# Decoder trunk: the loads and splits at three stage borders moved into the stage ahead of each

## The chip, the cores and the metric

The kernel runs on one core of a Trainium2 chip. The metric is the device time of one execution, in microseconds (us); lower is better. Engines are named as in the profile: PE (TensorE), DVE (VectorE), ACT (ScalarE), POOL (GpSimd) and SP, which here issues every DMA.

## The reference, cut to what matters

One layer of a decoder, for a prompt of 2048 rows and for 8 samples of 4 new rows each, with the same weights:

```python
h = rmsnorm(x, w['norm1_g'])
proj = jnp.einsum('nld,dc->nlc', h, w['w_in'])
qa, ka, va, qb, kb, vb, zc = jnp.split(proj, IN_SPLITS, axis=-1)
...
oc, s_fin = rwkv_mixer(zc, z_before, s0, w)      # the recurrence: token shift, decay, delta-rule state
mix = jnp.concatenate([oa.reshape(N, L, A_Q), ob.reshape(N, L, B_W), oc], axis=-1).astype(x.dtype)
x = x + jnp.einsum('nlc,cd->nld', mix, w['w_out'])
u = jnp.einsum('nld,df->nlf', rmsnorm(x, w['norm2_g']), w['mlp_up'])
x = x + jnp.einsum('nlf,fd->nld', jnp.square(jax.nn.relu(u)), w['mlp_down'])
```

The prompt's recurrence starts from a zero state and zero shift row; the samples' starts from `state_c_wkv` and `state_c_shift`.

## The kernel before

The program is a row of stages, each a block of its own: at its end every engine meets the others at a barrier, and SP reaches it only after its last stores have landed. The stages, with the profile's tile names:

1. `project`: the combined projection, written to `projT` and `vtok` in DRAM.
2. `prompt_attention`: attention heads of the prompt; results (`p_mo`) stored to `mixT` in DRAM.
3. A block of its own, `Era.clear` (L54 to L60): SP clears the 67 semaphores that stages 1 and 2 used, so that the later stages can have them.
4. `rwkv` with tag `cp`: the prompt's recurrence, in 8 segments of 256 tokens. Between its own steps the engines run the samples' attention (`SampleAttention`, "side"), whose cached keys and values come in 30 units of 768 KB through a ring of three buffers (`p_ring`).
5. `rwkv` with tag `cs`: the samples' recurrence, a single segment of 32 columns.
6. `out_project`: 17 row tiles times `w_out`, residual, norm, transpose.
7. `mlp`.

In stages 4 and 5 (L1956 to L1961) SP first issues the loads of the rows `z`, then of 14 constants (16 with the samples' row mask and state). All four compute engines wait at their start for every one of these loads (`c_in`), and all but DVE for DVE's preparation of `hbias`, `hka`, `omka` and `rko` as well (`zeroed`, L2001 to L2008). DVE's first consumers wait for POOL's `shift` (L1892, the difference of neighbouring tokens), which needs `z`. The order on each engine is written out by hand: `walk` calls `prepare` in pieces 0 to 10 (all ahead of the first group for segment 0), then `levels_of`, `hop` and `finish`; for the samples `special` follows `levels_of`.

In stage 6 every matmul of fp32 data is three matmuls on a high part (`mh`, `wh`, an ACT copy to fp32r) and a low part (`ml`, `wl`, a DVE subtraction). ACT and DVE split the weights `w_o` in two halves of 2 MB, and the first two tiles of `mixT` (`p_mix`), at the start of the stage, after SP has loaded them; PE waits for the first half (`w_low`).

Of the kernel before, what the change touches and what calls it, by code (L numbers as in the profile page):

```python
# [47 lines left out]
class Era(ExitStack):  # L48
# [351 lines left out]
def prompt_attention(nc, outer, projT, vtok, mask_w, mask_0, sinks, ident, mixT):  # L400
# [21 lines left out]
    with ExitStack() as ctx:  # L422
# [74 lines left out]
        def _(sp):  # L497
# [408 lines left out]
class SampleAttention:  # L906
# [5 lines left out]
    def __init__(self, nc, ctx, outer, projT, vtok, units, mask_b, mask_a, sink_a, ident, mixT):  # L912
        s = Scope(nc, ctx, outer)
        self.NR = NR = 3
        self.units, self.mixT = units, mixT
        self.ring = [s.sb(f"p3_ring{i}", [P, UNIT]) for i in range(NR)]
# [60 lines left out]
    def load_until(self, sp, slot):  # L977

        while self.next_unit < len(self.release):
# [7 lines left out]
            self.next_unit += 1  # L987

# [274 lines left out]
def rwkv(nc, outer, tag, sample, src, shift0, state0, cst, wts, mixT, col0, state_out, side=None):  # L1263
# [17 lines left out]
    with ExitStack() as ctx:  # L1281
        s = Scope(nc, ctx, outer)
        n_ = lambda x: f"{tag}_{x}"
        z = s.sb(n_("z"), [P, NZ, nb, nq + 1])
# [11 lines left out]
        sh0 = s.sb(n_("sh0"), [P, NZ, nb, 1]) if sample else None  # L1296
        znew = s.sb(n_("znew"), [P, NZ, W]) if sample else None
# [3 lines left out]
        par = s.sb(n_("par"), [P, 32])  # L1301
        omka = s.sb(n_("omka"), [P, NP3])
        hka = s.sb(n_("hka"), [P, NP3])
        hbias = s.sb(n_("hbias"), [P, 6])
        w2 = s.sb(n_("w2"), [P, 384])
        g2 = s.sb(n_("g2"), [P, 384])
        hones = s.sb(n_("hones"), [P, P])
        hmean = s.sb(n_("hmean"), [P, P])
        rko = s.sb(n_("rko"), [P, NP3, P])
        id64 = s.sb(n_("id64"), [P, HD])  # L1310
        mAB = s.sb(n_("mAB"), [P, 2, C])
        mT1 = s.sb(n_("mT1"), [P, C])
        mM1 = s.sb(n_("mM1"), [P, C])
        idU = s.sb(n_("idU"), [P, C])
        mL = s.sb(n_("mL"), [P, len(levels), C])
        scm = s.sb(n_("scm"), [P, W])
        cc = s.sb(n_("cc"), [P, 1])
        hsum = s.sb(n_("hsum"), [P, 32])
        hback = s.sb(n_("hback"), [96, NP3, P])
        ksum = s.sb(n_("ksum"), [96, W])  # L1320
        vsum = s.sb(n_("vsum"), [96, W])
        rm = s.sb(n_("rm"), [P, NB]) if sample else None
# [10 lines left out]
        S0 = s.sb(n_("S0"), [P, NS0, NP3, nb, HD])  # L1333
# [4 lines left out]
        c_in = s.sem(n_("c_in"))  # L1338
        z_in = s.sem(n_("z_in"))
        shift_in = s.sem(n_("shift_in")) if sample else None  # L1340
# [8 lines left out]
        consts = [(par[:, :], cst["par"]), (hsum[:, :], cst["hsum"]), (hback[:, :, :], cst["hback"]), (w2[:, :], wts["w2"]), (g2[:, :], wts["g2"]), (hones[:, :], cst["hones"]),  # L1349
                  (hmean[:, :], cst["hmean"]), (id64[:, :], cst["id64"]), (mAB[:, :, :], cst[tag + "AB"]),  # L1350
                  (mT1[:, :], cst[tag + "T1"]), (mM1[:, :], cst[tag + "M1"]), (idU[:, :], cst[tag + "I"]),
                  (mL[:, :, :], cst[tag + "L"]), (scm[:, :], cst[tag + "scan"])]
        if sample:
            consts += [(rm[:, :], cst["rowmask"]), (S0[:, 0], state0)]
# [247 lines left out]
        def scalar_walk(e):  # L1602
# [3 lines left out]
            def prepare(seg, i):  # L1606
# [1188 lines left out]
```

## Time and profile before

| | us |
|---|---|
| median of 3 runs | 3337.21 (3335.07 to 3338.07) |
| the profiled execution | 3336.69 |
| its span | 3334.9 |
| PE busy | 3066.4 (92%) |
| DVE busy | 1581.4 (47%) |
| ACT busy | 816.6 (24%) |
| POOL busy | 351.7 (11%) |

The profile is that of one execution. "Busy" is the sum of an engine's instructions; a row of the timeline says when a group of instructions starts, how long it lasts in all, and in brackets how long the engine had been idle and what ended that.

### The profile page before, as it was taken

How to read it: one execution, taken by the hardware profiler on the slowest of the kernel's cores; microseconds unless marked ns; L12 is line 12 of the kernel's file. 1: busy time of each engine (PE TensorE's matmuls, PEld its weight loads, DVE VectorE, ACT ScalarE, POOL GpSimd, SP SyncE). 2: the span in 40 equal slices, each digit the busy share in tenths (PEclk: the TensorE clock that was granted, in tenths of full speed). 3: DMA queues.
4: the chain of work that ended last, by engine and by line, in shares of the span. 5: the costliest groups of instructions: out<-in, count | busy, mean ns of one | idle time of the engine just before them, and what ended most of it. 6: DMA issues, size and time to landing. Idle time of an engine off the chain costs nothing. (4 is left out here: it accounts for less than half of the span.)

```text
span 3334.9 us, 65660 instructions
## 1 busy us (share of the span) xinstructions
PE 3066.4 (92%) x27080; PEld 2599.7 (78%) x27080; DVE 1581.4 (47%) x3057; ACT 816.6 (24%) x1500; POOL 351.7 (11%) x473
## 2 busy tenths in 40 slices
PE   7999999799589888875699799999999999999998
PEld 7999997466377777764487588888887988888887
DVE  6211121677466666742333444444446554444545
ACT  5000000565222333211222322111123211222112
POOL 4000000643232233210000000000000000000000
PEclk9999999899799999995799899999999999999999
DMA  4222121531322320001454511111113311111111
GB/s 149 71 71 71 68 84 48 156 104 36 98 86 82 117 82 25 7 12 30 142 173 147 182 51 50 50 50 33 42 51 105 131 51 50 50 37 39 50 45 65
DMA packets 145083, 249.58 MB, mean 75 GB/s; under 512 B 21952, under 2 KB 101920, under 8 KB 144096
## 3 DMA queue, kind: packets, MB, share of 16 engines
q1 hardware_dynamic: 144864, 246.41, 22.1%
q8 instruction: 167, 2.74, 0.3%
q14 instruction: 52, 0.43, 0.0%
HBM read 185.85 MB, written 60.52 MB: 74 GB/s over the span
## 5 line engine op out<-in xcount | busy, mean ns | idle before, releaser
L2639 DVE TENSOR_TENSOR m_y<-m_y,m_db 128x512 f32<-128x512 f32 x512 | 351.9, 688 | 324.4 <-PE m_db L2408 324.0
L2406 PE MATMUL m_ub<-m_hh,m_wuh 128*128 128x352 f32 (+1 forms) x1280 | 451.4, 353 | 19.4 <-DVE m_hl L2585 19.4
L2407 PE MATMUL m_ub<-m_hl,m_wuh 128*128 128x352 f32 (+1 forms) x1280 | 449.9, 351 | 0.0
L2408 PE MATMUL m_ub<-m_hh,m_wul 128*128 128x352 f32 (+1 forms) x1280 | 449.4, 351 | 0.0
L2406 PE MATMUL m_db<-m_wdh,m_uh 128*128 128x512 f32 x1024 | 407.3, 398 | 4.8 <-DVE m_wdl L2594 4.7
L2408 PE MATMUL m_db<-m_wdh,m_ul 128*128 128x512 f32 x1024 | 404.3, 395 | 0.0
L2407 PE MATMUL m_db<-m_wdl,m_uh 128*128 128x512 f32 x1024 | 403.2, 394 | 0.0
L186 PE MATMUL p_bank<-p_xh,p_wh 128*128 128x416 f32 x800 | 286.6, 358 | 11.8 <-DVE p_wl L307 11.8
L187 PE MATMUL p_bank<-p_xl,p_wh 128*128 128x416 f32 x800 | 283.8, 355 | 0.0
L188 PE MATMUL p_bank<-p_xh,p_wl 128*128 128x416 f32 x800 | 282.8, 353 | 0.0
L2406 PEld LDWEIGHTS m_ub<-m_hh,m_wuh 128*128 128x128 f32 x1280 | 241.0, 188 | 46.8 <-issue 13.1
L2407 PEld LDWEIGHTS m_ub<-m_hl,m_wuh 128*128 128x128 f32 x1280 | 241.4, 189 | 23.3
L2408 PEld LDWEIGHTS m_ub<-m_hh,m_wul 128*128 128x128 f32 x1280 | 241.0, 188 | 22.8
L2406 PEld LDWEIGHTS m_db<-m_wdh,m_uh 128*128 128x128 f32 x1024 | 192.7, 188 | 63.6 <-issue 19.4
L2607 DVE TENSOR_TENSOR m_sq<-m_r 128x352 f32<-128x352 f32 (+1 forms) x160 | 94.5, 590 | 294.0 <-ACT m_r L2503 294.0
L2408 PEld LDWEIGHTS m_db<-m_wdh,m_ul 128*128 128x128 f32 x1024 | 192.8, 188 | 46.1
L2407 PEld LDWEIGHTS m_db<-m_wdl,m_uh 128*128 128x128 f32 x1024 | 193.4, 189 | 44.6
L2528 ACT ACTIVATE m_wdh<-m_wdr 128x1024 fp32r<-128x1024 f32 x62 | 62.2, 1052 | 630.8 <-PE m_db L2408 630.8
L2503 ACT ACTIVATE m_r<-m_ub 128x352 f32<-128x352 f32 (+1 forms) x160 | 82.8, 517 | 449.4 <-PE m_ub L2408 438.2
L186 PEld LDWEIGHTS p_bank<-p_xh,p_wh 128*128 128x128 f32 x800 | 153.4, 192 | 14.3 <-DVE p_wl L307 12.2
L362 DVE TENSOR_TENSOR p_ob<-p_bank,p_rs 128x416 f32<-128x416 f32 x70 | 41.4, 592 | 256.0 <-PE p_bank L188 256.0
L188 PEld LDWEIGHTS p_bank<-p_xh,p_wl 128*128 128x128 f32 x800 | 152.2, 190 | 2.2
(394 smaller groups left out, 5047.8 us busy)
## 6 DMA issues: line engine op xcount, KB each, us to landing
m_wur<-w_up SPq DMA_DIRECT2D x64, 512.0 KB, 6.1
m_wdr<-w_dn SPq DMA_DIRECT2D x64, 512.0 KB, 4.3
p_ring<-units SPq DMA_DIRECT2D x30, 768.0 KB, 6.2
out_projT<-p_ob SPq DMA_DIRECT2D x100, 208.0 KB, 1.9
cp_z<-out_projT SPq DMA_DIRECT2D x8, 1408.0 KB, 7.8
p_wr<-w_fm SPq DMA_DIRECT2D x20, 512.0 KB, 3.6
p_mix<-mixT SPq DMA_DIRECT2D x16, 512.0 KB, 5.0
p_x<-x SPq DMA_DIRECT2D x16, 512.0 KB, 3.7
```

What stands on the lines that cost most here:

```text
L186: pe.matmul(out, wh_, mh, start=(k == 0), stop=False)
L187: pe.matmul(out, wh_, ml, start=False, stop=False)
L188: return pe.matmul(out, wl_, mh, start=False, stop=(k == KC - 1))
L362: dve.tensor_tensor(ob[gi][:, 0:TG], bank[gi][:, 0:TG], rs[:, cols(gi)], ALU.mult).then_inc(evac, 1)
L2406: pe.matmul(out, wh, mh, start=first, stop=False)
L2407: pe.matmul(out, wh, ml, start=False, stop=False)
L2408: return pe.matmul(out, wl, mh, start=False, stop=last)
L2503: act.activation(r[:, q, 0:n], ub[g][:, 0:n], ACT.Relu).then_inc(relued, 1)
L2528: act.activation(wdh[:, j], wdr[:, j], ACT.Copy).then_inc(wd_high, 1)
L2607: dve.tensor_tensor(sq[:, q, 0:n], r[:, q, 0:n], r[:, q, 0:n], ALU.mult).then_inc(u_sq, 1)
L2639: dve.tensor_tensor(yh, yh, db[(2 * a + h) % ND][:, :], ALU.add).then_inc(y_added, 1)
```

## The change

Three things move, and no arithmetic of the result changes.

- `RwkvShared` holds the prompt's first rows `z` and the constants that both recurrences use, in tiles of their own (`rw_...`). It is loaded by SP inside `prompt_attention`, when that stage has come to its last head pair. The samples' recurrence no longer loads or prepares constants again.
- The block that clears semaphores is gone. SP clears the 67 of stages 1 and 2 inside the prompt's recurrence, in its last segment (`stale.clear`). In the same place `SampleEarly` loads what the samples' recurrence needs of its own (state, rows, shift rows, seven small constants) into two ring buffers whose last units have been used.
- `OutWeights` loads `w_o` in eight parts, and the first two tiles of `mixT`, at the start of the samples' recurrence. ACT makes the high parts after its `prepare` pieces 6 to 9, DVE the low parts in `special`, between `vm` and `um`. `out_project` begins with these done; PE there waits for all eight parts.

```diff
@@ class Era
-    def clear(self):
-        with self.nc.Block() as block:
-            @block.sync
-            def _(sp):
-                for handle in self.held:
-                    sp.sem_clear(handle)
+    def clear(self, sp):
+        for handle in self.held:
+            sp.sem_clear(handle)
@@ prompt_attention, sync
                     load_k(u + 1)
                     load_v(u + 1)
+                else:
+                    shared.load(sp)
                 for c in range(NCL):
                     store(NCL * u + c)
@@ class SampleAttention
+    def load_early(self, sp):
+
+        for n, load in ((len(self.release) - 3, self.early.load_state), (len(self.release) - 2, self.early.load_rest)):
+            sem, count, _ = self.release[n]
+            sp.wait_ge(sem, count)
+            load(sp)
@@ rwkv, scalar_walk, prepare
                     S.done(e.activation(ksum[:, :], ksum[:, :], ACT.Sqrt), "sroot", seg)
+                if i in (6, 7, 8, 9) and ahead and not isinstance(e, Rehearsal):
+                    for k in (2 * i - 12, 2 * i - 11):
+                        ahead.high(e, k)
@@ rwkv, vector_walk, special
                     V.done(i, name, 0)
+                    if name == "vm" and ahead and not isinstance(e, Rehearsal):
+                        for k in range(KC):
+                            ahead.low(e, k)
@@ rwkv, sync
-            if sample:
-                sp.dma_start(znew[:, :, :], src[:, :, SEQ:T].rearrange("z p t -> p z t")).then_inc(z_in, 16)
-                sp.dma_start(sh0[:, :, :, :], shift0).then_inc(shift_in, 16)
-            else:
-                sp.dma_start(z[:, :, 0, 1:nq + 1], src[:, :, 0:W].rearrange("z p t -> p z t")).then_inc(z_in, 16)
-            for dst, src_ in consts:
-                sp.dma_start(dst, src_).then_inc(c_in, 16)
+            if ahead:
+                ahead.load(sp)
...
                     side.load_until(sp, PIECES * (seg - 1) + 1)
+                if side and seg == nseg - 1:
+                    side.load_early(sp)
+                    stale.clear(sp)
@@ class OutWeights
+    def load(self, sp):
+        for k in range(KC):
+            sp.dma_start(self.wr[:, k, :], self.w_o[:, k, :]).then_inc(self.w_in[k], 16)
+        for t in range(2):
+            sp.dma_start(self.m[t][:, :, :], self.mixT[:, :, P * t:P * (t + 1)].rearrange("k p n -> p k n")).then_inc(self.mix_in[t], 16)
+
+    def high(self, act, k):
+        act.wait_ge(self.w_in[k], 16)
+        act.activation(self.wh[:, k, :], self.wr[:, k, :], ACT.Copy).then_inc(self.w_high, 1)
+        if k < 2:
+            act.wait_ge(self.mix_in[k], 16)
+            act.activation(self.mh[k][:, :, :], self.m[k][:, :, :], ACT.Copy).then_inc(self.m_high, 1)
```

How SP's program reads. Before, between the last stores of the attention (`mixT<-p_mo`) and the first loads of the recurrence stand the 67 clears and the branches of three borders:

```order
L531 DMA mixT<-p_mo 128x512 x8
L422 UNCONDITIONAL_BRANCH
L57 UNCONDITIONAL_BRANCH
L60 ISA x67
L56 UNCONDITIONAL_BRANCH
L1949 UNCONDITIONAL_BRANCH
L1959 DMA cp_z<-out_projT 128x11x256
L1961 DMA cp_par<-cst_par 128x32
```

After the change the loads of `z` and the constants stand four stores earlier (the rest of the constants is left out between these two pieces), and the samples' attention's own loads (`p_qa` to `p_ident`, 16 of them) are the first of the new stage:

```order
L528 DMA mixT<-p_mo 128x512 x4
L2048 DMA cp_z<-out_projT 128x11x256
L2050 DMA rw_par<-cst_par 128x32
```

```order
L2050 DMA cp_scm<-cst_cpscan 128x256
L528 DMA mixT<-p_mo 128x512 x4
L419 UNCONDITIONAL_BRANCH
L1937 UNCONDITIONAL_BRANCH
L974 DMA p_qa<-out_projT 64x32 x4
L974 DMA p_qb<-out_projT 128x3x32
```

What moved: 15 loads went ahead of the border, 67 clears and two borders are gone from it. The clears now stand, with ten small loads ahead of them, between the fifth and the sixth of the recurrence's eight stores (`mixT<-cp_yc`).

ACT's program in the samples' recurrence, after the change, from the square root of `prepare` piece 5 to the first copies of `levels_of`:

```order
L1615 ACT_TABLE_LOAD
L1615 ACTIVATE cs_ksum<-cs_ksum 96x32
L2146 ACTIVATE p_wh<-p_wr 128x1024
L2149 ACTIVATE p_mh<-p_mix 128x1024
L2146 ACTIVATE p_wh<-p_wr 128x1024
L2149 ACTIVATE p_mh<-p_mix 128x1024
L2146 ACTIVATE p_wh<-p_wr 128x1024 x6
L1648 ACTIVATE cs_tok<-cs_q 32x192 x6
```

Before, `cs_tok` followed `cs_ksum` directly; ten copies now stand between them, the second of which waits for a tile of `mixT` that SP loads after all eight parts of `w_o`.

DVE's program in `special`, after the change:

```order
L1844 TENSOR_TENSOR cs_vm<-cs_tok,p_ring 32x512 x6
L2153 TENSOR_TENSOR p_wl<-p_wr,p_wh 128x1024
L2156 TENSOR_TENSOR p_ml<-p_mix,p_mh 128x1024
L2153 TENSOR_TENSOR p_wl<-p_wr,p_wh 128x1024
L2156 TENSOR_TENSOR p_ml<-p_mix,p_mh 128x1024
L2153 TENSOR_TENSOR p_wl<-p_wr,p_wh 128x1024 x6
L1844 TENSOR_TENSOR cs_um<-cs_uu,p_ring 32x512 x6
```

Before, `cs_um` followed `cs_vm`; ten subtractions now stand between them.

## Rows read from the trace of the kernel before

**Rows 1.** The page, busy time of the engines.

```profile
PE 3066.4 (92%) x27080; PEld 2599.7 (78%) x27080; DVE 1581.4 (47%) x3057; ACT 816.6 (24%) x1500; POOL 351.7 (11%) x473
```

**Rows 2.** Timeline, attention to prompt's recurrence: start, length, instructions [idle <-releaser].

```profile
866.34 0.32 SPq L531 DMA_DIRECT2D mixT<-p_mo  x1
...
873.35 0.39 SPq L1959 DMA_DIRECT2D cp_z<-out_projT  x1
...
884.57 0.17 DVE L2001 TENSOR_SCALAR cp_hbias<-cp_par 128x6 f32<-128x6 f32 x1 [18.26 <-issue]
...
885.62 4.88 POOL L1892 TENSOR_TENSOR cp_zs<-cp_z 128x2816 f32<-128x2816 f32 x1 [27.78 <-DVE cp_rko L2007]
```

**Rows 3.** Waits of SP's queue: us in total, times, longest us.

```profile
SPq L556 <- DMA mixT<-p_mo: 1.7, 1, 1.7
...
SPq L1281 <- DMA out_state_s<-cs_S: 2.9, 1, 2.9
...
SPq L1953 <- DVE cp_yc L1788: 221.2, 7, 67.8
```

**Rows 4.** Timeline, first segment of the prompt's recurrence.

```profile
889.59 1.38 SPq L986 DMA_DIRECT2D p_ring<-units  x3
...
895.35 0.38 SPq L1968 DMA_DIRECT2D cp_z<-out_projT  x1
...
904.12 4.88 POOL L1892 TENSOR_TENSOR cp_zs<-cp_z 128x2816 f32<-128x2816 f32 x1 [6.33 <-DMA cp_z<-out_projT]
...
907.78 0.42 ACT L1632 ACTIVATE cp_ksum<-cp_ksum 96x256 f32<-96x256 f32 x1
...
909.74 1.74 DVE L1744 RECIPROCAL cp_ksum<-cp_ksum 96x256 f32<-96x256 f32 x1
```

**Rows 5.** Line L1741, all its instructions: ns min/median/max.

```profile
L1741 DVE TENSOR_TENSOR cp_tA<-cp_kp,cp_zs x8: 944/1142/4017, 905.8 to 1395.2; 128x768 f32<-128x768 f32 x8
```

**Rows 6.** Timeline, prompt's to samples' recurrence, and the samples' first steps.

```profile
1505.61 0.37 SPq L1956 DMA_DIRECT2D cs_znew<-out_projT  x1
...
1518.40 0.17 DVE L2001 TENSOR_SCALAR cs_hbias<-cs_par 128x6 f32<-128x6 f32 x1 [18.03 <-issue]
...
1519.51 0.70 DVE L2011 MEMSET cs_am<- 128x768 f32 x1 [0.23 <-DVE cs_rko L2007]
1520.12 0.19 DVE L1704 COPY cs_z<-cs_sh 128x88 f32<-128x88 f32 x1
...
1531.76 0.23 ACT L1632 ACTIVATE cs_ksum<-cs_ksum 96x32 f32<-96x32 f32 x1
...
1540.07 2.01 ACT L1662 ACTIVATE cs_tok<-cs_q 32x192 f32<-32x192 f32 x6 [8.08 <-PE cs_q L1533]
```

**Rows 7.** Lines of the splits in `project`, the same shapes: ns min/median/max.

```profile
L292 ACT ACTIVATE p_wh<-p_wr x16: 1059/1060/1061, 104.5 to 450.7; 128x1024 fp32r<-128x1024 f32 x16
L365 DVE TENSOR_TENSOR p_wl<-p_wr,p_wh x14: 1224/1225/1226, 133.7 to 429.0; 128x1024 fp32r<-128x1024 f32 x14
```

**Rows 8.** Timeline, samples' recurrence to output projection.

```profile
1563.79 3.78 DVE L1859 TENSOR_TENSOR cs_um<-cs_uu,cs_rm 32x512 f32<-32x512 f32 x6 [15.59 <-ACT cs_uu L1681]
...
1601.42 0.48 SPq L1982 DMA_DIRECT2D out_state_s<-cs_S  x1
...
1605.21 0.37 SPq L2097 DMA_DIRECT2D p_mix<-mixT  x1
1605.30 0.06 DVE L2191 MEMSET p_eps<- 128x1 f32 x1 [4.33 <-PEq L1281]
...
1619.52 3.62 ACT L2172 ACTIVATE p_wh<-p_wr 128x4096 fp32r<-128x4096 f32 x1 [1.34 <-DMA p_wr<-w_o]
...
1622.78 0.76 PE L2151 MATMUL p_acc<-p_wh,p_mh 128*128 128x512 f32 x1 [23.44 <-DVE p_wl L2202]
```

**Rows 9.** The page, DMA issues: KB each, us to landing.

```profile
cp_z<-out_projT SPq DMA_DIRECT2D x8, 1408.0 KB, 7.8
```

**Rows 10.** A window's length, then PE, PEld, DVE, ACT, POOL busy (count), then granted clock, DMA share, GB/s.

```profile
1605.00:1622.00 17.00, 0.00 (x0) 0.00 (x0) 5.08 (x3) 7.15 (x3) 0.00 (x0) 0.50 0.94 357
```

More of the change, by code:

```diff
@@ L2045, in rwkv_constants, with __init__, staging, load @@
     return out
-def out_project(nc, outer, mixT, xtok, w_o, g2, ident, x2, h2T):
+class OutWeights:
+    def __init__(self, nc, ctx, outer, mixT, w_o):
+        s = Scope(nc, ctx, outer)
+        self.wh = s.sb("p5_wh", [P, KC, D], F32R)
+        self.wl = s.sb("p5_wl", [P, KC, D], F32R)
+        self.m = [s.sb(f"p5_mix{i}", [P, KC, P]) for i in range(2)]
+        self.mh = [s.sb(f"p5_mh{i}", [P, KC, P], F32R) for i in range(2)]
+        self.ml = [s.sb(f"p5_ml{i}", [P, KC, P], F32R) for i in range(2)]
+        self.w_in = [s.sem(f"p5_w_in{i}") for i in range(KC)]
+        self.w_high = s.sem("p5_w_high")
+        self.w_low = s.sem("p5_w_low")
+        self.mix_in = [s.sem(f"p5_mix_in{i}") for i in range(2)]
+        self.m_high = s.sem("p5_m_high")
+        self.m_low = s.sem("p5_m_low")
+        self.mixT, self.w_o = mixT, w_o
+    def staging(self, nc, ctx, outer):
+        self.wr = Scope(nc, ctx, outer).sb("p5_wr", [P, KC, D])
+    def load(self, sp):
+        for k in range(KC):
[8 more added lines that the diff above has]
+            act.activation(self.mh[k][:, :, :], self.m[k][:, :, :], ACT.Copy).then_inc(self.m_high, 1)
+    def low(self, dve, k):
+        dve.wait_ge(self.w_high, k + 1)
+        dve.tensor_tensor(self.wl[:, k, :], self.wr[:, k, :], self.wh[:, k, :].bitcast(F32), ALU.subtract).then_inc(self.w_low, 1)
+        if k < 2:
+            dve.wait_ge(self.m_high, k + 1)
+            dve.tensor_tensor(self.ml[k][:, :, :], self.m[k][:, :, :], self.mh[k][:, :, :].bitcast(F32),
+                               ALU.subtract).then_inc(self.m_low, 1)
+def out_project(nc, outer, ahead, mixT, xtok, g2, ident, x2, h2T):
     NT = SEQ // P + 1
@@ L2053, in out_project @@
         s = Scope(nc, ctx, outer)
-        WP = 2
-        wr = [s.sb(f"p5_wr{i}", [P, KC // WP, D]) for i in range(WP)]
-        wh = s.sb("p5_wh", [P, KC, D], F32R)
-        wl = s.sb("p5_wl", [P, KC, D], F32R)
+        wh, wl, m, mh, ml = ahead.wh, ahead.wl, ahead.m, ahead.mh, ahead.ml
+        w_low, mix_in, m_high, m_low = ahead.w_low, ahead.mix_in, ahead.m_high, ahead.m_low
         g = s.sb("p5_g", [P, KC])
@@ L2139, in turn @@
                 tr.then_inc(turned, 1)
+            pe.wait_ge(w_low, KC)
             for t, (r0, n) in enumerate(tiles):
@@ new lines, in decoder_trunk @@
+    with Era(nc) as outer, Era(nc) as base, Era(nc) as first:
+        with ExitStack() as common:
+            project(nc, first, A["xT"], A["g1"], A["cst_ones"], A["w_fm"], A["w_v"], A["projT"], A["vtok"])
+            shared = RwkvShared(nc, common, base, cst, wts, zc)
+            prompt_attention(nc, first, A["projT"], A["vtok"], A["cst_mask_w"], A["cst_mask_0"], A["sinks"],
+                             A["cst_ident"], mixT, shared)
+            with ExitStack() as ring:
+                early = SampleEarly(nc, ring, base, cst, zc, A["shift0"], A["state0"])
+                with ExitStack() as kept:
+                    side = SampleAttention(nc, kept, outer, early, A["projT"], A["vtok"], A["units"], A["cst_mask_b"],
+                                           A["cst_mask_a"], A["sink_a"], A["cst_ident"], mixT)
+                    rwkv(nc, outer, "cp", False, zc, shared, early, mixC, 0, A["state_p"], side, stale=first)
+                first.close()
+                with ExitStack() as kept:
+                    ahead = OutWeights(nc, kept, outer, mixT, A["w_o"])
+                    with ExitStack() as raw:
+                        ahead.staging(nc, raw, outer)
+                        rwkv(nc, outer, "cs", True, zc, shared, early, mixC, SEQ, A["state_s"], ahead=ahead)
+                    out_project(nc, outer, ahead, mixT, A["x"], A["g2"], A["cst_ident"], x2, h2T)
```

197 lines of the change are left out of this document (102 added, 95 removed).

## Prediction

> **What bounds the kernel now.** I read the page first, then the timelines around the borders, and last the waits of SP's queue. The reader is to see in [rows 1] that PE is busy for 92% of the span, so 3334.9 - 3066.4 = 268 us are all that a better order can give back without shorter matmuls. The timelines show where three pieces of these lie. From the last store of the attention at 866.34 to POOL's first step of the recurrence at 885.62 no engine has work except SP with its loads [rows 2]. The prompt's and the samples' recurrence are parted in the same way, with DVE idle for 18.03 us [rows 6]. At the start of the output projection PE waits 23.44 us for the first split weights [rows 8]. All three are exposed: every later stage starts after them, and none has other work to run. So what is taken from them comes off the end, as long as nothing new ends last there.
>
> The sum is made against the profiled execution, 3336.69 us, which is 1.8 us more than its span and 0.5 us under the median of 3337.21. What it gives is taken off the median.
>
> **Border 1, attention to the prompt's recurrence.** What stays: the last store is issued at 866.34 + 0.32 = 866.66 and SP waits 1.7 us for it [rows 3], to 868.36. What a bare border costs is read at the one between samples and output projection: state stored at 1601.42 + 0.48, 2.9 us of waiting [rows 3], so landed at 1604.80; DVE's first instruction at 1605.30 [rows 8], 0.50 later. So DVE can start at 868.86. It now starts at 884.57, because of the 67 clears and their block (868.36 to 873.35, 5.0 us) and then 15 loads [rows 2]. DVE's preparation of the constants stays on the path as it is: 884.57 to POOL's start at 885.62 is 1.05 us, before and after. Gain 884.57 - 868.86 = **15.7 us**.
>
> The loads themselves go to the attention's last head pair. There SP issues them (15 at some 0.5 us, worked out below) ahead of a store for which it waits anyway, and they are hidden there. The clears and ten loads go to the last segment of the recurrence: 5.0 us for the clears, and at most 0.65 us for each load by the issue times of 0.37 to 0.48 us seen for single loads and stores [rows 6, 8], so under 12 us. SP's queue waits there for the next result to store, 221.2 us over seven stores and up to 67.8 us at once [rows 3]. I cost them at nothing; without that cover it would be those 12 us. The two waits ahead of the loads are for ring units that are used up several slots before SP comes there, by the release table, so they don't hold it either.
>
> A second effect is on what SP issues next. From 873.35 [rows 2] to 889.59 [rows 4] it issued 31 loads, 15 of the recurrence and 16 of the samples' attention, 0.52 us each. Now it comes to the latter at 868.8, and to the first three ring units at 868.8 + 16 x 0.52 = 877.2, 12.4 us earlier than before, while the recurrence starts 15.7 us earlier: relative to it they are 3.3 us late. The second segment's `z` is issued at 895.35 - 15.7 = 879.6, right behind them. Before, from the issue of the units to the landing of `z` at 904.12 were 14.5 us [rows 4]; the same bytes queued again give 891.7. Counted in the old times (15.7 added) that is 907.4, 3.3 us later than POOL's second `shift` started. That is no loss: nobody needs this shift before the first level. It is rather a gain. DVE's `rkp` (L1741) starts at 905.8 and took 4.02 us, against 0.94 us for the shortest of the eight [rows 5], since POOL's shift of 4.88 us ran from 904.12 and DVE was done 0.8 us after its end. With the shift from 907.4 on, `rkp` is over by 906.8, and the reciprocal behind it starts when ACT's root is ready, at 907.78 + 0.42 = 908.2, instead of 909.74 [rows 4]. PE's next step waits for that reciprocal. Gain **1.5 us**. Bounds: if the shift comes before 905.8 it is as before, 0; if it comes later than about 909, it can hold a two-input step of DVE further down, for at most its 4.88 us less what the row above shows as free, some 2 us lost. I take 1.5.
>
> The Trainium skill (SBUF — State Buffer, "SBUF: two separate sides") says why: a DVE instruction with two SBUF inputs and a GpSimd instruction that reads SBUF exclude each other for the whole instruction, and whoever comes second waits. The 4.02 us fit that. By the rule a shift that landed between 908.2 and 913 would not hurt the reciprocal, which has one input; without the rule, if any DVE work were held, the reciprocal would lose up to 4 us and the sum be 5.5 us worse in this place.
>
> **Border 2, prompt's to samples' recurrence.** The border itself stays: SP comes through at 1505.61 [rows 6], DVE 0.09 us later by 1605.21 and 1605.30 [rows 8], so at 1505.70. Gone are 18 loads and DVE's constants. What is left is the memset of `am` and then the first copy, 1519.51 to 1520.12 = 0.61 us. The copy starts at 1506.3 instead of 1520.12 [rows 6]: gain **13.8 us**.
>
> Against it stands new work on ACT. The chain up to the square root is unchanged and ends at 1531.76 + 0.23 - 13.8 = 1518.2. Then ACT makes eight high parts of 1.06 us each [rows 7] and two of the `mixT` tiles, of the same shape; the next copy on the chain, `cs_tok`, was due at 1540.07 - 13.8 = 1526.3. Ten copies are 10.6 us: even if all had landed ACT would come at 1528.8, 2.5 us late. The loads: before, 0.5 MB of `mixT` and 4.2 MB of weights, 4.7 MB, were issued from 1605.21 and ended ACT's wait at 1619.52 [rows 8], 14.3 us; the window gives 357 GB/s [rows 10]. Now 4.2 MB of weights come first from 1505.61, then the two tiles. The first tile completes the same 4.7 MB, at about 1505.6 + 14.7 = 1520.3, the second 1.5 us later, at 1521.8. So ACT: first part to 1519.3, waits for the tile, 1520.3 to 1521.4, second part to 1522.4, second tile to 1523.5, six more to 1529.9. That is **3.6 us** late, and the PE, DVE and ACT steps behind `cs_tok` are chained, so all of it shows. Bounds: 2.5 if nothing is waited for; 16.3 if the loads went at the 1408 KB in 7.8 us of the `z` loads [rows 9], 185 GB/s, which would bring the second tile in at 1535.
>
> DVE's low parts: 8 x 1.225 + 2 x 1.23 = 12.3 us [rows 7], behind `vm`. DVE sat idle for 15.59 us there, until ACT's `uu` [rows 8], while PE did its products with the state. 3.3 us are left over, so 0. If they started late by more than 3.3 us, the excess would come on the path. The high parts are all there by then. Border 2 gives 13.8 - 3.6 = **10.2 us**.
>
> **Border 3, samples to output projection.** PE needs `w_low`, `m_low` and the border: it can start with DVE at about 1605.4 in the old times, instead of 1622.78 [rows 8], gain **17.4 us**. The granted clock is 0.50 (1.2 GHz) there before [rows 10], after 17 us without PE work and behind the thin products of the samples; it will be so after the change, so the first matmuls are as long as before and nothing is lost or won by it. The rows of `x` are now SP's first loads, and due only when tile 0 is through, some 14 us later.
>
> **Sum.** 15.7 + 1.5 + 10.2 + 17.4 = 44.8 us; 3337.2 - 44.8 = **3292.4 us**, -1.3%.
>
> **The rivals.**
> 1. *The splits take the samples' chain over.* ACT has only the 8.08 us in which it stood idle for `cs_tok` [rows 6], and one late tile holds all eight parts, since the second copy waits for it. With the loads at 185 GB/s ACT is 16.3 us late instead of 3.6, the result 3305. Against it: 357 GB/s with the same tensors. 11%.
> 2. *A stage's start is not free.* Before, PE, ACT and POOL had 15 us at each border in which to get to their first real instruction; only DVE and SP were seen to start at once. If the others need 2 us at each of the three, it is 3298. For it: nothing but that no row shows the contrary; against it DVE's 0.50 us. 10%.
> 3. *SP's queue becomes the bound, and the kernel slower than before.* Clears and small loads stand ahead of three stores in the last segment, and DVE can't write `yc` again until the store ahead has landed. SP has 67.8 us of room before one of them [rows 3]; to cost more than the 44.8 us won, the block would have to take over 112 us, against my 12. The price at 120 us would be 3337.2 - 44.8 + 52 = 3345. Each of the 67 clears would have to take 1.6 us; all of them and two borders took 5.0. 2%.
> 4. *The change doesn't do what it says:* some other load or wait that came along with the constants ends last, and the stages start when they did. Then 3336. At border 1 all loads are issued a head pair ahead, so I see none. 2%.
>
> My forecast has the other 75%.
>
> **How the numbers follow.** The likeliest sum is 3292.4. Its own spread: shift and DVE -2 to +1.5 us, ACT's lateness 1 us less or some more, and the granted clock, which drops for a few us at the starts of stages in ways that shift with their timing, some 5 us either way. That gives 3285 to 3300; with most of rival 2 and the near part of rival 1 I take 3285 to 3301. A measurement of this kernel can tell about 0.2% (6.7 us) from no change. Faster by more than that: forecast and rivals 1 and 2, 96%; within: 2%; slower: 2%.
>
> **What would show it.** Right: DVE's first instruction of the recurrence 0.5 us after the last store has landed; POOL's shift 1.05 us later; `rkp` of the first segment near 0.95 us; the first copy of the samples some 0.7 us after SP's first load of `w_o`; `cs_tok` waiting for no PE, ACT busy without a gap ahead of it but one of about a microsecond for `p_mix`; DVE's `um` still waiting for ACT's `uu`; PE's first `p_acc` product within 0.6 us of DVE's memset. Wrong: `um` behind the low parts, `cs_tok` over 5 us late, SP's store of `yc` waited for, or engines that stand at a border with "issue" as the reason.

## The result and the profile after

| | median of the timed runs, us | profiled execution, us | its span, us |
|---|---|---|---|
| before | 3337.64 (3335.07 to 3342.72, 4 runs) | 3336.69 | 3334.9 |
| after | 3284.76 (3282.53 to 3289.92, 4 runs) | 3283.62 | 3281.8 |

The ratio is 0.9834, interval 0.9816 to 0.9852: 53 us faster, where the prediction took off 44.8. The 3284.76 lie 0.24 us outside its range of 3285 to 3301. The changed kernel was timed in two other sets of runs, against 3334.97 and 3339.59 of the kernel before: 48.4 and 49.5 us faster (e9, e12 below). So the prediction was short by some 4 to 8 us, and all on one side.

The page, busy time, answers to [rows 1]. PE is busy for 6 us less, though it runs the same 27080 instructions:

```profile
PE 3060.3 (93%) x27080; PEld 2597.7 (79%) x27080; DVE 1576.7 (48%) x3056; ACT 817.3 (25%) x1506; POOL 351.1 (11%) x473
```

The timeline after, attention to the prompt's recurrence and its first segment, answers to [rows 2, 4] (start, length, instructions, idle and releaser):

```profile
863.65 0.32 SPq L528 DMA_DIRECT2D mixT<-p_mo  x1
...
866.20 0.07 DVE L1989 MEMSET cp_z<- 128x11 f32 x1 [2.58 <-PEq L419]
866.23 0.17 DVE L1991 TENSOR_SCALAR rw_hbias<-rw_par 128x6 f32<-128x6 f32 x1
...
867.26 4.88 POOL L1880 TENSOR_TENSOR cp_zs<-cp_z 128x2816 f32<-128x2816 f32 x1 [12.10 <-DVE rw_rko L1995]
...
874.49 1.38 SPq L985 DMA_DIRECT2D p_ring<-units  x3
876.99 0.38 SPq L1951 DMA_DIRECT2D cp_z<-out_projT  x1
...
887.44 0.94 DVE L1726 TENSOR_TENSOR cp_tA<-cp_kp,cp_zs 128x768 f32<-128x768 f32 x1
...
889.42 0.42 ACT L1615 ACTIVATE cp_ksum<-cp_ksum 96x256 f32<-96x256 f32 x1
889.87 1.75 DVE L1729 RECIPROCAL cp_ksum<-cp_ksum 96x256 f32<-96x256 f32 x1 [1.49 <-ACT cp_ksum L1615]
890.19 4.88 POOL L1880 TENSOR_TENSOR cp_zs<-cp_z 128x2816 f32<-128x2816 f32 x1 [10.77 <-DMA cp_z<-out_projT]
```

From the attention's last store to POOL's first step are 867.26 - 863.65 = 3.61 us, before 19.28. The second shift now starts behind `rkp` (L1726), which takes 0.94 us in place of 4.02, and the reciprocal starts 0.03 us after ACT's root is through.

The timeline after, prompt's to samples' recurrence, answers to [rows 6]:

```profile
1486.33 4.05 SPq L2140 DMA_DIRECT2D p_wr<-w_o  x8
...
1486.63 0.70 DVE L1998 MEMSET cs_am<- 128x768 f32 x1 [5.54 <-PEq L1287]
1487.24 0.19 DVE L1689 COPY cs_z<-p_ring 128x88 f32<-128x88 f32 x1
...
1498.84 0.23 ACT L1615 ACTIVATE cs_ksum<-cs_ksum 96x32 f32<-96x32 f32 x1
1498.97 1.04 ACT L2146 ACTIVATE p_wh<-p_wr 128x1024 fp32r<-128x1024 f32 x1
1500.89 1.06 ACT L2149 ACTIVATE p_mh<-p_mix 128x1024 fp32r<-128x1024 f32 x1 [0.88 <-DMA p_mix<-mixT]
1501.86 1.04 ACT L2146 ACTIVATE p_wh<-p_wr 128x1024 fp32r<-128x1024 f32 x1
1502.80 1.04 ACT L2149 ACTIVATE p_mh<-p_mix 128x1024 fp32r<-128x1024 f32 x1
1503.75 5.77 ACT L2146 ACTIVATE p_wh<-p_wr 128x1024 fp32r<-128x1024 f32 x6
1509.42 1.99 ACT L1648 ACTIVATE cs_tok<-cs_q 32x192 f32<-32x192 f32 x6
```

ACT is busy without a gap from its root to `cs_tok` but for the 0.88 us for `p_mix`, and comes to `cs_tok` with no wait for PE: it is late. From the copy to `cs_tok` are 22.18 us, before 19.95, so late by 2.23.

The timeline after, samples' recurrence to output projection, answers to [rows 8]:

```profile
1533.13 1.28 DVE L1844 TENSOR_TENSOR cs_um<-cs_uu,p_ring 32x512 f32<-32x512 f32 x2 [4.11 <-ACT cs_uu L1667]
...
1574.55 0.82 SPq L2205 DMA_DIRECT2D p_x<-x  x2
1574.63 0.06 DVE L2282 MEMSET p_eps<- 128x1 f32 x1 [4.32 <-PEq L1287]
...
1574.75 0.76 PE L2247 MATMUL p_acc<-p_wh,p_mh 128*128 128x512 f32 x1 [6.06 <-PEq L1287]
```

DVE's `um` still waits for ACT, by 4.11 us after the low parts, and PE starts 0.12 us behind DVE's memset, where it stood still for another 17.4.

SP in the last segment: the clears, and its waits for results to store (line, us in total, times, longest), answer to [rows 3]:

```profile
L57 SPq EVENT_SEMAPHORE_RANGE_CLEAR  x67: 25/30/49, 1338.8 to 1343.0; - x67
```
```profile
SPq L1941 <- DVE cp_yc L1773: 209.9, 7, 56.7
```

They took 4.2 us, and SP still had 56.7 us of waiting in one piece; it came right behind them, as the next store was issued at 1399.8.

Where the 53.1 us of the two profiled executions lie, each as the difference between two points of the two timelines:

| stretch | predicted | shown |
|---|---|---|
| up to the attention's last store (SP's 15 loads stand ahead of its last four stores) | 0 | 2.69 |
| border 1, store to DVE's first instruction | 15.7 | 15.68 |
| first segment, POOL's shift to the reciprocal | 1.5 | 1.51 |
| rest of the prompt's recurrence | 0 | -0.6 |
| border 2, SP's first load to the first copy | 13.8 | 13.60 |
| ACT late at `cs_tok` | -3.6 | -2.23 |
| border 3, SP's first load to PE's first product | 17.4 | 17.37 |
| **inside the output projection** | **0** | **5.7** |
| last stage, its border, the rest | 0 | -0.6 |

The only large one that the prediction has not is inside the output projection. Its matmuls are the same but for the places of their tiles; the splits of the second half of the weights, which ran beside its first matmuls before, are gone from it (e2 below keeps them). The groups of its first pass (ns min/median/max, first and last start), before and after:

```profile
L2151 PE MATMUL p_acc<-p_wh,p_mh x272: 388/394/764, 1622.8 to 1828.0; 128*128 128x512 f32 x128, 128*32 128x512 f32 x8
```
```profile
L2247 PE MATMUL p_acc<-p_wh,p_mh x272: 389/389/763, 1574.7 to 1774.3; 128*128 128x512 f32 x128, 128*32 128x512 f32 x8
```

The same 272 matmuls take 205.2 us before and 199.6 after. Two stretches of 18 matmuls further in, at the full clock, before and after:

```profile
1628.04 0.51 PE L2151 MATMUL p_acc<-p_wh,p_mh 128*128 128x512 f32 x1
...
1631.64 0.39 PE L2151 MATMUL p_acc<-p_wh,p_mh 128*128 128x512 f32 x1
...
1635.84 0.39 PE L2151 MATMUL p_acc<-p_wh,p_mh 128*128 128x512 f32 x1
```
```profile
1577.44 0.51 PE L2247 MATMUL p_acc<-p_wh,p_mh 128*128 128x512 f32 x1
...
1581.69 0.39 PE L2247 MATMUL p_acc<-p_wh,p_mh 128*128 128x512 f32 x1
...
1585.77 0.39 PE L2247 MATMUL p_acc<-p_wh,p_mh 128*128 128x512 f32 x1
```

They are 4.20 / 18 = 0.2333 us apart before and 4.08 / 18 = 0.2267 after. The median busy time of one, 394 and 389 ns, tells the same by halves; the distance of the starts is what counts, since neighbours overlap. Over the stage's 816 matmuls the means are 0.2332 and 0.2275 us, which makes 4.7 us. The rest, about 1 us, is how long the clock stayed at its lower level: the granted clock is 0.50 (1.2 GHz) at the start of the stage in both, with PE idle for 23.44 us ahead of it before and 6.06 after, and the matmuls start 0.43 us apart. The first row of each fence is the first product at the full clock (granted 0.99), 5.3 us behind the stage's first before and 2.7 us after. That 1 us is no effect of the change that these runs could show. In the 14 profiled executions of this study the stretch lasted from 2.69 to 6.11 us, in three of the changed kernel alone 2.69, 3.55 and 4.40, and e4, with PE idle for 32 us ahead of it, has 4.86.

### The profile page after: what moved, and what is told of

The parts are those of the page before. It is cut to its first block and busy times, and to the rows that moved or that the text cites. A ratio compares the mean times of both kernels' runs of the same rounds, so it can differ in the third digit from the quotient of the medians.

```text
span 3281.8 us, 65652 instructions
## 1 busy us (share of the span) xinstructions
PE 3060.3 (93%) x27080; PEld 2597.7 (79%) x27080; DVE 1576.7 (48%) x3056; ACT 817.3 (25%) x1506; POOL 351.1 (11%) x473
```

## The experiments

From here on "the distance" is that between the starts of two matmuls of 512 columns that follow each other.

**The place of the tiles (e1, e2).** In SBUF the weights' high part `p5_wh` lies at byte 49280 before and 57664 after, the tile `p5_mh0` at 123584 and 131392. Modulo 4096 that is 128 and 704 before, 320 and 320 after. e1 puts the changed kernel's tiles where they were, modulo 4096:

```diff
+        s.sb("p5_pad0", [P, 976])
         self.wh = s.sb("p5_wh", [P, KC, D], F32R)
 ...
+        s.sb("p5_pad1", [P, 144])
         self.m = [s.sb(f"p5_mix{i}", [P, KC, P]) for i in range(2)]
```

e2 does the reverse to the kernel before: its three small tiles move behind the large ones, and with that `wh`, `wl`, `mh` and `ml` all lie at 128 modulo 4096.

```diff
-        g = s.sb("p5_g", [P, KC])
-        idt = s.sb("p5_ident", [P, P])
-        eps = s.sb("p5_eps", [P, 1])
 ...
         ml = [s.sb(f"p5_ml{i}", [P, KC, P], F32R) for i in range(2)]
+        g = s.sb("p5_g", [P, KC])
+        idt = s.sb("p5_ident", [P, P])
+        eps = s.sb("p5_eps", [P, 1])
```

> The changed kernel, with two unused tiles in SBUF (3904 and 576 bytes per partition) ahead of p5_wh and of p5_mix0, so that wh, wl, mh and ml of the output projection stand at the same addresses modulo 4096 bytes as in the kernel before (128 for the weights, 704 for the mixT tiles; in the changed kernel all stand at 320). Theory P (the place of the two operands sets the time of a matmul): the start-to-start distance of the 512-column matmuls of p_acc goes back from 0.227 us to 0.233 us and the output projection is 5 us longer, 3290 us in all; everything else as in the changed kernel. Theory R (the 5 us are chance of that one execution or come from something else that the change did to the stage): 0.227 us stays, 3285 us.

> The kernel before, with p5_g, p5_ident and p5_eps allocated behind ml instead of ahead of mixT's tiles, so that wh, wl, mh and ml all stand at 128 modulo 4096 bytes; nothing else differs. Theory P, if the relation of the two operands counts: p_acc's distance falls from 0.233 to 0.227 us, the output projection is 5 us shorter, 3332 us in all. If the address itself counts (320 against 128): 0.233 us and 3337 us. Theory R: 3337 us too.

The first pass of both (e1, then e2):

```profile
L2249 PE MATMUL p_acc<-p_wh,p_mh x272: 391/394/763, 1573.4 to 1779.1; 128*128 128x512 f32 x128, 128*32 128x512 f32 x8
```
```profile
L2151 PE MATMUL p_acc<-p_wh,p_mh x272: 389/389/764, 1626.6 to 1826.9; 128*128 128x512 f32 x128, 128*32 128x512 f32 x8
```

e1 takes 205.7 us again, at 0.2333 us from start to start, and e2 200.3 at 0.2275. So the place alone moves the 4.7 us, in either kernel and both ways; what else the four stages differ by is the time at the lower clock, 6.1 us in e1 and 3.6 in e2. In the total (the kernel before took 3345.01 us beside them): e1 3290.21 us (3285.58 to 3294.32), ratio 0.9843 [0.9821, 0.9864]; e2 3335.62 (3328.27 to 3347.42), ratio 0.998 [0.9963, 0.9996]. Two medians 5 us apart would settle little here; the distance in the trace does.

**The rule (e5).** A stage of its own between output projection and last stage runs 71 blocks of 24 matmuls on zeros, with only the operands' offsets different; all that the kernel computes otherwise stays. It was executed once.

```diff
+        runs += [[(d, 0)] for d in range(0, 256, 8)]
+        runs += [[(0, d)] for d in range(0, 256, 16)]
+        runs += [[(0, 0), (d, 0)] for d in range(16, 256, 16)]
+        runs += [[(d, 0), (d, 0), (d + 128, 0)] for d in range(0, 128, 16)]
 ...
+            for n, run in enumerate(runs):
+                for i in range(24):
+                    a, b = run[i % len(run)]
+                    pe.matmul(banks[n % 2][:, :], sta[:, a:a + P], mov[:, b:b + 512], start=(i == 0), stop=(i == 23))
```

> The changed kernel with one stage added between the output projection and the last stage: 71 blocks of 24 matmuls of 512 columns on operands full of zeros, nothing else running. Within the first 32 blocks only the place of the stationary operand moves against the moving one, in steps of 32 bytes from 0 to 992; the other blocks move the moving operand, or change between two stationary places. The stage adds about 71 x 24 x 0.23 = 392 us. Theory that the distance between matmuls depends on where the stationary operand lies against the moving one: the block at 0 bytes shows 0.227 us from start to start, the one at 64 bytes 0.233 us (those are the two kernels' offsets in the output projection, and both of their distances). Rival, that the slower distance came from other engines and DMAs that write and read near the operands at the same time: all blocks alike, at or under 0.227 us. Second rival, that only where each operand itself lies counts: the blocks that move the stationary operand and those that move the moving one by the same bytes differ from each other.

Stretches of the blocks with the stationary operand 64, 192 and 256 bytes on (start, time of all, and their count):

```profile
1804.64 5.06 PE L2368 MATMUL t_bank<-t_mov,t_sta 128*128 128x512 f32 x21
...
1827.06 4.97 PE L2368 MATMUL t_bank<-t_mov,t_sta 128*128 128x512 f32 x21
...
1838.15 4.92 PE L2368 MATMUL t_bank<-t_mov,t_sta 128*128 128x512 f32 x21
```

Less the length of the last one, 0.39 us, and divided by 20 that is 0.2335, 0.2290 and 0.2265 us. Over the last 16 of each block the means are:

| stationary less moving, bytes modulo 256 | 0 | 32 | 64 | 96 | 128 | 160 | 192 | 224 |
|---|---|---|---|---|---|---|---|---|
| stationary moved | 0.2267 | 0.2333 | 0.2333 | 0.2343 | 0.2333 | 0.2336 | 0.2289 | 0.2333 |
| moving moved | 0.2267 | | 0.2333 | | 0.2329 | | 0.2287 | |

The row repeats itself every 256 bytes, four times over the 1024 that were tried, to 0.2 ns. (The very first block, at half clock, is left out.) So the theory holds and is sharpened: as long as it stays the same from one matmul to the next, the offset between the two operands modulo 256 bytes sets the distance. The two kernels' numbers, 0.2333 at 64 and 0.2267 at 0, are in the row. Contention with other engines falls, since nothing else ran in these blocks (a DMA share of 0.00, DVE and POOL at 0), and so does the rival by which each operand's own place counts: moving either gives the same, within 0.4 ns. Where the stationary operand alternates between two places the rule isn't enough. Between 0 and 256 bytes the distance is 0.2267, as it should be. But between 0 and 64 it is 0.2325 and between 0 and 320 it is 0.2300, though 64 and 320 are the same modulo 256; between 0 and 128 it is 0.2326 and between 0 and 384 it is 0.2333. By the row, the mean of the two distances would be 0.2300 in all four cases. So already here a matmul's own offset is not all that counts.

**The last stage's operands (e7, e8, e10, e11).** There the distance is 0.2320 us in the mean, with rows of 4224 bytes, which is 128 modulo 256: every second pair lies 128 bytes apart. e7 shifts the stationary weights of the up projection and the moving ones of the down projection by 128 bytes for every second row, and takes groups of 384, 384 and 288 columns:

```diff
-              Half(1, SEQ // 2, [(0, 352), (352, 352), (704, 352)], True, FFB, NSUP * NU, FFB * 2)]
+              Half(1, SEQ // 2, [(0, 384), (384, 384), (768, 288)], True, FFB, NSUP * NU, FFB * 2)]
 ...
+        up_at = lambda w, j, k: w[:, 1056 * j + 544 * ((k + 1 + j) % 2) + P * (k // 2):1056 * j + 544 * ((k + 1 + j) % 2) + P * (k // 2) + P]
+        down_at = lambda w, j, lo=0, hi=D: w[:, 1056 * j + lo:1056 * j + hi]
```

e8 orders them as well: `ks = [0, 2, 4, 6, 1, 3, 5, 7]` in place of `range(KC)`, and `js = (1, 0) if b % 2 else (0, 1)`.

> The changed kernel with only the last stage's operands placed anew, so that the stationary and the moving operand of every matmul of that stage lie at the same place modulo 256 bytes (before, 128 bytes apart in every second pair); the groups of the second half are 384, 384 and 288 columns instead of three of 352, so that their starts are multiples of 256 bytes too. The order of the matmuls is kept, so that the pair's common place changes from one k to the next. Theory that only the offset between the two operands of one matmul counts: every 512-column matmul of the stage goes to 0.227 us (from 0.2321 in the mean over 4608), 21 us off the total, 3264 us. Rival, that a matmul also depends on the next one's stationary operand, which lies 128 bytes off at each third matmul here: the distance stays about 0.230, 8 to 12 us off. Null: the placement of the last stage is not worth anything, 3284 us.

> The kernel of e7_mlp_aligned with the matmuls also ordered so that the common place modulo 256 bytes changes only once in 24 matmuls of the up projection and once in 6 of the down projection (even k ahead of odd k, and the two blocks in turn first). By either theory of e7 the distance of the 512-column matmuls is 0.227 to 0.228 us: 19 to 21 us off the changed kernel's total, 3264 to 3266 us, 0.978 of the kernel before. Null: 3284 us, 0.983.

> The changed kernel itself, on the chip of e7 and e8, so that these are compared with it there. 0.983 to 0.985 of the kernel before; its attention stage ends within 863 to 868 us as in the other executions of the same code, the output projection takes 200 to 201 us from its first to its last matmul.

e7 was 3287.53 us (3283.34 to 3292.97), ratio 0.986 [0.9838, 0.9883], e8 3277.87 (3273.48 to 3284.97), 0.9836 [0.9816, 0.9856], the changed kernel beside them 3286.62 (3279.26 to 3294.06), 0.9858 [0.9836, 0.9879]. In e7 nothing was won. The distances show why: in each k of its up projection they were 0.2308, 0.2267 and 0.2325 us. Only the middle one, with no change of the common place near it, is fast; the two around the change from one k to the next are slow. So "only the offset within one matmul" is wrong: the matmul ahead and the one behind count as well. (In the down projection, where the common place changes too, the distance was 0.2323 against 0.2319.) In e8, with the change once in 24, 21 of 24 are at 0.2266 to 0.2268. The down projection, where the change still comes once in 6, is at 0.2300. The forecast of 19 to 21 us for e8 took that for fast, and was too high by half: from its first up product to the end of the span the stage took 1477.5 us against 1487.8 in e9.

e10 gives the rows of `m_uh` and `m_ul` 4352 bytes (17 x 256), so that the down projection has one place throughout; e11 is e10 with the old groups of 352.

```diff
-        uh = s.sb(n_("uh"), [P, 2, SUP, W], F32R)
-        ul = s.sb(n_("ul"), [P, 2, SUP, W], F32R)
+        uh = s.sb(n_("uh"), [P, 4352], F32R)
+        ul = s.sb(n_("ul"), [P, 4320], F32R)
+        u_at = lambda u, par, j, lo, hi: u[:, 1088 * (2 * par + j) + lo:1088 * (2 * par + j) + hi]
```

> The changed kernel with the last stage's operands placed so that the pair of every matmul there lies at the same place modulo 256 bytes, and so that this common place is one and the same through the whole down projection (rows of m_uh and m_ul 4352 bytes apart instead of 4224) and changes once in 24 matmuls of the up projection (even k ahead of odd k); groups of 384, 384 and 288 columns in the second half. From e8: up projection 0.2271 us (1536 matmuls, 0.0051 each, 7.8 us), down projection now 0.227 us too (3072 matmuls, 0.0049 each, 15 us), the narrower groups 1.3 us the other way: 21 to 22 us off the changed kernel's total. Rival, that writes of other engines near the operands hold the down projection up and not its placement (it went only from 0.2319 to 0.2300 in e8): it stays at 0.230 us and the total falls by 12 us.

> The kernel of e10_all_384 with the three groups of 352 columns of the changed kernel, whose middle one starts 128 bytes off modulo 256. By the placement theory its 768 matmuls lie 128 bytes apart from their stationary operands and stay slow, the other 1536 get faster: within 2 us of e10. 20 to 23 us off the changed kernel's total.

> The changed kernel itself, on the chip of e10 and e11, so that they are compared with it there: 0.983 to 0.986 of the kernel before, 20 to 22 us above e10.

The down projection's first pass, of the changed kernel and of e10:

```profile
L2491 PE MATMUL m_db<-m_wdh,m_uh x1024: 389/397/695, 1853.2 to 3271.2; 128*128 128x512 f32 x171
```
```profile
L2496 PE MATMUL m_db<-m_wdh,m_uh x1024: 389/389/727, 1855.2 to 3253.7; 128*128 128x512 f32 x171
```

1418.0 us from first to last against 1398.5. The distance is 0.2269 in the down and 0.2271 in the up projection. e10 was **3266.36 us** (3261.63 to 3271.96), ratio 0.9784 [0.9761, 0.9806]; e11 3271.11 (3263.53 to 3274.55), 0.9789 [0.9766, 0.9812]; the changed kernel beside them 3290.11 (3284.61 to 3295.89), 0.9857 [0.9834, 0.988]. So e10 is faster than both kernels, by 73 and by 24 us, with the same number of matmuls; its last stage takes 1468.6 us where the changed kernel's takes 1487.9.

e11's last stage took 1469.4 us, but its forecast for the narrow groups came out the other way round. The two outer groups, whose operands are congruent, went to 0.1609 and 0.1606 us and got slower than the 0.1590 of the changed kernel, where half of the pairs lie 128 bytes apart; the middle group, where all pairs do, is the fastest with 0.1586. So for 352 columns the offset 0 is not the fast one.

**The constants late (e3).** The loads of `RwkvShared` are issued at the start of the prompt's recurrence instead of in the attention:

```diff
-                else:
-                    shared.load(sp)
 ...
             if ahead:
                 ahead.load(sp)
+            else:
+                shared.load(sp)
```

> The changed kernel, but z and the 14 shared constants are loaded at the start of the prompt's recurrence again, ahead of the samples' attention's loads. The clears stay where the change put them. From SP's first load to DVE's start it was 11.2 us before; now it is 0.1. Expected: DVE starts 11.1 us later than in the changed kernel, and the second shift comes early enough, relative to rkp, to hold it again (rkp about 4 us, 1.5 us on the path): +12.6 us, 3297 us. If the loads had been hidden in some other way: under +5 us. If the lock on two-input DVE steps is not real: rkp 0.95 us and +11.1 us.

```profile
878.66 0.17 DVE L1991 TENSOR_SCALAR rw_hbias<-rw_par 128x6 f32<-128x6 f32 x1 [13.57 <-issue]
...
879.68 4.88 POOL L1878 TENSOR_TENSOR cp_zs<-cp_z 128x2816 f32<-128x2816 f32 x1 [23.07 <-DVE rw_rko L1995]
...
897.52 4.88 POOL L1878 TENSOR_TENSOR cp_zs<-cp_z 128x2816 f32<-128x2816 f32 x1 [5.67 <-DMA cp_z<-out_projT]
...
899.87 3.35 DVE L1724 TENSOR_TENSOR cp_tA<-cp_kp,cp_zs 128x768 f32<-128x768 f32 x1
903.14 1.74 DVE L1727 RECIPROCAL cp_ksum<-cp_ksum 96x256 f32<-96x256 f32 x1
```

POOL's first step comes 879.68 - 865.12 = 14.56 us after the attention's store instead of 3.61. And `rkp` is held again: it starts 2.35 us behind POOL's shift and ends at 903.22, 0.82 behind its end. Before it was done 0.8 us after the shift's end too, though it had started 1.68 us behind the shift's start. Only part of the 1.5 us comes back with it: from POOL's first step to the reciprocal are 23.46 us, against 24.12 in the kernel before and 22.61 in the changed one, as the second shift lies 0.66 us earlier behind the first here than before. The Trainium skill (SBUF — State Buffer, "SBUF: two separate sides") has the two exclude each other for the whole instruction, with the DVE instruction's two inputs in SBUF; the traces agree, three times: held in the kernel before and here, not held after. And the reciprocal, which has one input, ran for 1.75 us beside POOL's shift in the changed kernel against 1.74 alone. In the total e3 is 3300.58 us (3299.64 to 3302.61), ratio 0.9872 [0.9854, 0.989]; 3297 was expected, and the changed kernel's three medians are 3284.76, 3286.62 and 3290.11.

**The splits late (e4).** The loads of `w_o`, and all splits, stand at the start of the output projection again (but in eight pieces, and ahead of the two tiles, as the change has them):

```diff
-    rwkv(nc, outer, "cs", True, zc, shared, early, mixC, SEQ, A["state_s"], ahead=ahead)
+    rwkv(nc, outer, "cs", True, zc, shared, early, mixC, SEQ, A["state_s"])
 ...
+            ahead.load(sp)
             load_x(0)
 ...
+            for k in range(KC):
+                ahead.high(act, k)
```

> The changed kernel, but w_o and the first two mixT tiles are loaded and split at the start of the output projection (in the same eight parts and the same order), not in the samples' recurrence. Expected: cs_tok is no longer late (2.3 us back), PE's first p_acc product comes 17.4 us after the border plus what eight parts and the late mixT tiles cost, about 23 us in all: +17 to +23 us, likeliest +21, 3306 us. If the splits in the samples' recurrence cost what they save, as one rival has it: within 5 us of the changed kernel. The places of wh and mh are those of the changed kernel, so p_acc stays at 0.227 us by theory P.

The memset, `cs_tok`, and the output projection's start:

```profile
1485.89 0.70 DVE L1998 MEMSET cs_am<- 128x768 f32 x1 [5.56 <-PEq L1287]
...
1506.40 2.00 ACT L1648 ACTIVATE cs_tok<-cs_q 32x192 f32<-32x192 f32 x6 [8.08 <-PE cs_q L1516]
...
1571.62 0.06 DVE L2285 MEMSET p_eps<- 128x1 f32 x1 [4.33 <-PEq L1287]
...
1586.38 1.06 ACT L2149 ACTIVATE p_mh<-p_mix 128x1024 fp32r<-128x1024 f32 x1 [9.82 <-DMA p_mix<-mixT]
...
1597.83 0.29 PEld L2248 LDWEIGHTS p_acc<-p_wh,p_mh 128*128 128x128 f32 x1 [32.30 <-DVE p_wl L2153]
```

`cs_tok` comes 20.51 us after the memset, and waits 8.08 us for PE as before the change; with the splits it is 22.79. So the splits cost the samples' chain 2.28 us. They save more here than the 17.4 of border 3: 26.2 us from memset to PE, where about 23 were expected, because the second piece's copy stands behind a tile whose load is behind all weights. 3309.23 us (3300.8 to 3312.96), ratio 0.9896 [0.9871, 0.9922].

**The tiles first (e6).** In `OutWeights.load` the two loads of `mixT` are issued ahead of the eight of `w_o`.

```diff
     def load(self, sp):
+        for t in range(2):
+            sp.dma_start(self.m[t][:, :, :], self.mixT[:, :, P * t:P * (t + 1)].rearrange("k p n -> p k n")).then_inc(self.mix_in[t], 16)
         for k in range(KC):
             sp.dma_start(self.wr[:, k, :], self.w_o[:, k, :]).then_inc(self.w_in[k], 16)
-        for t in range(2):
-            sp.dma_start(self.m[t][:, :, :], self.mixT[:, :, P * t:P * (t + 1)].rearrange("k p n -> p k n")).then_inc(self.mix_in[t], 16)
```

> The changed kernel with the two loads of mixT tiles issued ahead of the eight loads of w_o, instead of behind them. Theory that ScalarE comes late to its copy of cs_tok by the sum of its split copies and by 0.88 us of waiting for p_mix: the wait ahead of the first p_mh is gone, cs_tok starts 0.9 us sooner against the stage's start (22.8 us after the memset of cs_am's partner, the first shift's copy, was 22.8 in the changed kernel; now 21.9), and the total falls by 0.9 us, less than can be measured. Rival, that the lateness is set by the copies' own length behind the root alone, and a wait for w_o's pieces takes the place of that for p_mix: cs_tok starts where it did, within 0.3 us.

```profile
1489.40 0.70 DVE L1998 MEMSET cs_am<- 128x768 f32 x1 [5.54 <-PEq L1287]
...
1502.69 1.04 ACT L2149 ACTIVATE p_mh<-p_mix 128x1024 fp32r<-128x1024 f32 x1
...
1511.21 1.99 ACT L1648 ACTIVATE cs_tok<-cs_q 32x192 f32<-32x192 f32 x6
```

21.81 us from memset to `cs_tok`: the wait for the tile is gone, and 0.98 us of the 2.28. What is left, 1.30, is the ten copies. One run, 3285.55 us, says nothing of a microsecond.

## Why the prediction fell short

**Right.** All three borders, to 0.2 us each: 15.68 for 15.7, 13.60 for 13.8, 17.37 for 17.4. What they were worked out from, a border that costs DVE 0.50 us after the last landing, was 0.53 at the first and 0.50 at the third. At the second it was 0.70: DVE came 0.30 us behind SP there and not 0.09, which is the 0.2 us that this border gave less. Rival 2 (a stage's start is not free) is out: PE started 0.12 us behind DVE, and POOL's shift 1.03 us behind DVE's first constant, where it was 1.05. The lock in the first segment went by its steps: shift behind `rkp`, 0.94 us, reciprocal right at the root; 1.51 for 1.5, and e3 brought back 0.85 of it together with the shift's place. The clears and loads in the last segment cost nothing, with 56.7 us of SP's waiting left: rival 3 is out. Rival 4 (the change does not do it) too. DVE's low parts were hidden, with 4.1 us to spare where 3.3 were expected.

**Mis-sized.** "That is **3.6 us** late": ACT was late by 2.23, and e4 puts the price at 2.28. The copies were counted at 1.06 us each by their busy time, but start 0.946 us after one another, since each begins before the one ahead of it ends (six of them end 5.77 us after the first's start: 5 x 0.946 + 1.04). That is 1.0 us over ten. The wait for the first tile was 0.88 us in place of 1.0, and the first copy began inside the root's instruction in the same way, which is the rest. Rival 1 (the splits take the chain over) asked for the loads to be at 185 GB/s, and they weren't: the eight parts and the first tile, 4.7 MB, were there 14.56 us after SP's first load (1500.89 - 1486.33), 14.7 being expected.

**The step that failed.** "So the first matmuls are as long as before and nothing is lost or won by it": the sum has no term for the output projection. Behind that stands the assumption, not spelled out, that a stage whose instructions are the same takes the same time. It gave 5.7 us. e1, e2 and e5 show 4.7 us of it as the distance of its 816 matmuls, 0.2332 to 0.2275 in the mean (0.2267 in undisturbed stretches), set by where `wh` and `mh` lie against each other: 576 bytes apart modulo 4096 before, which is 64 modulo 256, and 0 after. The other microsecond is the time at the lower clock, which differed about as much between three executions of the changed kernel. The diff shows that the tiles are allocated elsewhere, so the difference of offsets could have been had before the run; the price of it could not, from the trace of before alone. With it the sum is 44.8 + 1.4 + 4.7 = 50.9 us, against 52.9, 48.4 and 49.5 in the three comparisons.

**Chance.** The attention's last store lay at 866.3 us in the profiled execution before and at 863.7 in the one after; in the twelve others of this study it was from 864.5 to 867.9. From there to the recurrence's last store the kernels with the change's first part need 612.6 to 622.3 us. So a single comparison of two traces can be off by several us, up to 10 in the recurrence, that are no effect of the change; the 2.69 us of the table's first row are of that kind. That is why the steps are judged by the table of stretches and the distances and not by the total. And that the median of 3284.76 lies 0.24 us outside the range is chance as well, since the changed kernel's two other medians, 3286.62 and 3290.11, lie inside; the missing 4.7 us are not.

**Open.** What inside PE or SBUF makes 256 bytes count is not shown by any of these runs; nor whether other types than fp32r, or other widths, have the same period. Of 384 columns and less only a few mean distances are known: 0.1739 (384) and 0.1315 (288) in e10, and those of 352 above, which do not follow the row for 512 columns. How the neighbours count is known only for the cases that were run.

## What to carry to other kernels

A border between stages costs what is issued and cleared in it: put the loads of the next stage's constants and first operands into the last waits of the stage ahead, and price each border from its last landing to DVE's first instruction, here 0.5 to 0.7 us. After any change to allocations, compare the distance of matmul starts in stages whose code did not change; where the two operands of a long row of fp32r matmuls of 512 columns lie apart by other than a multiple of 256 bytes, a pad of a few bytes was worth 2 to 3% of their time here, as long as the common place did not change from one matmul to the next. For 352 columns it was worth nothing, so measure it for each width. When copies are queued in a gap of another chain, count them from start to start, not by their busy time.

## What the runs showed of the hardware that was not expected

- The distance of fp32r matmuls of 128 x 128 by 512 columns at the full clock goes from 0.2267 to 0.2343 us with the offset between stationary and moving operand, with a period of 256 bytes (e5, each offset held for 24 matmuls); 0 is the fastest of the eight offsets tried, 192 (0.2289) the second.
- With both operands of every matmul congruent but the common place changed by 128 bytes from one k to the next, the two distances at the change are 0.2325 and 0.2308 (e7); so the neighbours count. With one operand alternating, 0 and 64 bytes give 0.2325, 0 and 320 bytes 0.2300 (e5).
- At 352 columns the order is another: 0.1609 and 0.1606 us with congruent operands, 0.1586 with the operands 128 bytes apart (e11).
- At the start of the same stage the granted clock stayed at 0.50 for 2.69 to 6.11 us in 14 executions, and for 2.69 to 4.40 in three of one kernel.
- 67 clears of semaphores took 4.2 us of SP's queue.
